# Nine panels on unnormalised x: the first norm's factor applied where the results are read

## The reference, cut to what matters

```
h = rms_norm(x, mix_norm_g)      # x * rsqrt(mean(x*x) + 1e-6) * g
proj = h @ w_in                  # 1024 x 7424
y_a = short_conv_mixer(proj[sc]); y_b = stick_breaking_attention(proj[sb])
y_c = rwkv7_mixer(proj[rw]);      y_d = spatial_gating(proj[sg])
gates = sigmoid(proj[gate] + gate_b)
```

## Time and profile before

| | us |
|---|---|
| median of three runs | 1012.99 |
| the profiled execution, whole | 1011.81 |
| its span, first to last instruction | 1010.0 |
| TensorE busy | 985.8 |
| VectorE busy | 695.9 |
| ScalarE busy | 537.2 |
| GpSimd busy | 35.5 |

### The profile page before, as it was taken

One profiled execution on the slowest core, in us unless ns is written; L12 is line 12 of the kernel. 1 busy time (PEld: TensorE's weight loads), 2 busy tenths in 40 slices (PEclk: granted clock), 3 DMA queues, 4 the chain that ended last, 5 costly groups with the idle time before them and its releaser, 6 DMA issues.

```text
span 1010.0 us, 20599 instructions
## 1 busy us (share of the span) xinstructions
PE 985.8 (98%) x8640; PEld 955.7 (95%) x8640; DVE 695.9 (69%) x855; ACT 537.2 (53%) x689; POOL 35.5 (4%) x28
## 2 busy tenths in 40 slices
PE   6998999999999999998999999999999999999998
PEld 5998898998999999998999999999999899999998
DVE  5678754655788988899886755556777867555553
ACT  5465645445565545466655444443676765435432
POOL 0035050000000000000000000000000000000000
PEclk9999999999999999999999999999999999999999
DMA  7643433332745555545333555555543135565551
GB/s 275 214 169 117 164 98 117 122 127 86 277 168 192 185 208 199 176 167 209 126 126 126 209 192 202 188 182 192 209 145 140 51 126 201 179 207 204 168 206 42
DMA packets 24833, 168.97 MB, mean 167 GB/s; under 512 B 2752, under 2 KB 3264, under 8 KB 4800
## 3 DMA queue, kind: packets, MB, share of 16 engines
q1 hardware_dynamic: 24192, 165.82, 46.9%
q10 hardware_dynamic: 576, 2.20, 0.6%
HBM read 166.96 MB, written 1.05 MB: 166 GB/s over the span
## 4 chain that ended last, share of the span: by engine, by line
PE 80%; DVE 13%; ACT 4%; issue 2%; DMA 0%; DVEq 0%; ACTq 0%
PE G L594 14%; PE G L595 13%; PE G L596 13%; PE D L594 8%; PE D L595 8%; PE D L596 8%; DVE wlo L1792 5%; PE M L595 2%; PE M L594 2%; PE M L596 2%; ACT whi L1275 2%; PE M L811 1%; PE D L1134 1%; PE D L1203 1%; PE M L641 1%
## 5 line engine op out<-in xcount | busy, mean ns | idle before, releaser
L1792 DVE TENSOR_TENSOR wlo<-raw,whi 128x2048 fp32r<-128x2048 f32 x155 | 354.2, 2290 | 125.7 <-ACT whi L1275 125.5
L594 PE MATMUL G<-xh,whi 128*128 128x256 f32 x1280 | 362.7, 283 | 4.4 <-DVE xl L1813 2.9
L595 PE MATMUL G<-xl,whi 128*128 128x256 f32 x1280 | 356.0, 278 | 0.0
L596 PE MATMUL G<-xh,wlo 128*128 128x256 f32 x1280 | 355.9, 278 | 0.0
L1275 ACT ACTIVATE whi<-raw 128x2048 fp32r<-128x2048 f32 x155 | 295.5, 1909 | 57.6 <-PE D L596 47.5
L594 PEld LDWEIGHTS G<-xh,whi 128*128 128x128 f32 x1280 | 241.8, 189 | 12.4 <-DVE wlo L1792 7.0
L595 PEld LDWEIGHTS G<-xl,whi 128*128 128x128 f32 x1280 | 241.6, 189 | 1.3 <-issue 1.2
L596 PEld LDWEIGHTS G<-xh,wlo 128*128 128x128 f32 x1280 | 241.5, 189 | 0.0
L594 PE MATMUL D<-hh,whi 128*128 128x256 f32 x672 | 185.8, 276 | 0.6 <-issue 0.6
L595 PE MATMUL D<-hl,whi 128*128 128x256 f32 x672 | 185.6, 276 | 0.0
L596 PE MATMUL D<-hh,wlo 128*128 128x256 f32 x672 | 185.6, 276 | 0.0
(11 more groups left out here) (398 smaller groups left out, 1383.5 us busy)
## 6 DMA issues: line engine op xcount, KB each, us to landing
raw<-wall_dram SPq DMA_DIRECT2D x155, 1024.0 KB, 4.9
x<-x_dram SPq DMA_DIRECT2D x4, 256.0 KB, 5.4
mem<-mem_dram ACTq DMA_DIRECT2D x1, 1024.0 KB, 4.8
out_dram<-x SPq DMA_DIRECT2D x4, 256.0 KB, 2.2
poolw<-pool_w_dram ACTq DMA_DIRECT2D x1, 768.0 KB, 6.3
cst<-cst_dram SPq DMA_DIRECT2D x1, 448.0 KB, 12.6
lora<-lora_dram SPq DMA_DIRECT2D x1, 256.0 KB, 11.9
sgw<-sg_w_dram SPq DMA_DIRECT2D x1, 256.0 KB, 12.7
```

Of the source, the lines that this page charges most:

```text
L594: mm(out, w_h, hi, start=start, stop=False, skip_group_check=skip)
L595: mm(out, w_h, lo, start=False, stop=False, skip_group_check=skip)
L596: return mm(out, w_l, hi, start=False, stop=stop, skip_group_check=skip)
L1792: signal(tt(wlo[:, pan.slot, 0:w], raw[:, pan.slot, 0:w], f32(whi[:, pan.slot, 0:w]), SUB), "w_lo")
```

## The change

The list starts with `gain` instead of `norm 0`. `gain` splits x * g (not x * g * rstd) into `gh` and `gl`, and panels 0 to 8 (rw, sc, sg) use these. The factor is applied when a result is read: for rw in a new VectorE step `rw_in`, in place after ScalarE's copy; for sc and sg by `read` on VectorE in place of ScalarE's copy. Squares are made after the splits, added on VectorE (`add_squares`, three instructions) and summed over channels by two fp32 products on TensorE. `root 0` comes after half of panel 1. The normalised x, which panels 9 and on still use, is made in five steps `norm_x` placed after panels 4 to 8. The load of panel 0 goes ahead of the four loads of x. `warm_start` runs first on TensorE. Three loads of constants share a semaphore, and some buffers move.

```diff
-    W = [("norm", 0)] + [("panel", PAN["rw"] + i) for i in range(4)]
-    W += [("rw_low",), ("panel", PAN["sc"]), ("rw_gates",), ("panel", PAN["sc"] + 1), ("rw_cum",), ("rw_square",),
-          ("panel", PAN["sc"] + 2), ("panel", PAN["sg"]), ("rw_key",), ("panel", PAN["sg"] + 1), ("rw_scale",), ("rw_mix",),
+    W = [("gain",), ("panel", PAN["rw"]), ("begin", PAN["rw"] + 1), ("root", 0), ("rw_in", 0)]
+    for i in range(1, 4):
+        W += [("panel", PAN["rw"] + i), ("rw_in", i)]
+    W += [("rw_low",), ("panel", PAN["sc"]), ("norm_x", 0), ("rw_gates",), ("panel", PAN["sc"] + 1), ("norm_x", 1), ("rw_cum",),
+          ("rw_square",), ("panel", PAN["sc"] + 2), ("norm_x", 2), ("panel", PAN["sg"]), ("norm_x", 3), ("rw_key",),
+          ("panel", PAN["sg"] + 1), ("norm_x", 4), ("rw_scale",), ("rw_mix",),
...
-    XLN = {"rw": 4, "wo": 8, ...
+    XLN = {"sb": 4, "wo": 8, ...
+    GAINED = ("rw", "sc", "sg")
+    SCALED = ("sc", "sg", "in0m", "kv")
...
+        load(Pan(0), A["wall"][0])
         for i in range(4):
             sp.dma_start(x[:, 2 * i:2 * i + 2, :], A["x"][:, 2 * i:2 * i + 2, :]).then_inc(S(f"x_moved{i}"), 16)
-        for p in range(SLOTS):
+        for p in range(1, SLOTS):
             load(Pan(p), A["wall"][p])
...
 # TensorE
+        def gained_panel(out, pan):
+            for i in range(4):
+                pe.wait_ge(S("gain_l"), i + 1)
+                for k in (2 * i, 2 * i + 1):
+                    for n in range(2):
+                        ins = tile3(out[:, n, :], pan, n * KT + k, P, gh[:, k, :], gl[:, k, :],
+                                    k == 0 and n == 0, k == KT - 1, skip=True)
+            return ins
...
-                for k in range(KT):
-                    pe.wait_ge(S("sq"), k // 2 + 1)
-                    ins = mm(M[1][:, 0, :], ones, wk[:, k, :], start=k == 0, stop=k == KT - 1)
+                ins = summed(M[1][:, 0, :], wk, "sq_sum", 0)
...
 # ScalarE
+        def gain():
+            split_to(1)
+            act.wait_ge(S("ld_par"), 16)
             for i in range(4):
+                act.wait_ge(S(f"x_moved{i}"), 16)
+                for k in (2 * i, 2 * i + 1):
+                    ins = fn(gh[:, k, :], x[:, k, :], ACT.Copy, scale=pcol("mix_g", k))
+                signal(ins, "gain_h")
+            split_to(2)
+            squares(0)
+
+        def norm_x(i):
+            if i < 4:
+                act.wait_ge(S("nrm"), i + 1)
                 signal(fn(xh[:, 2 * i:2 * i + 2, :], wk[:, 2 * i:2 * i + 2, :], ACT.Copy), "xh")
...
 # VectorE
+        def gain():
+            split_to(1)
+            for i in range(4):
+                dve.wait_ge(S("gain_h"), i + 1)
+                for k in (2 * i, 2 * i + 1):
+                    ins = stt(gl[:, k, :], x[:, k, :], pcol("mix_g", k), f32(gh[:, k, :]), MUL, SUB)
+                signal(ins, "gain_l")
+            split_to(2)
+            for i in (1, 2, 3):
+                add_squares(wk, "sq", 0, i, 3, "sq_sum")
+
+        def norm_x(i):
+            if i < 4:
+                scaled(wk, x, rstd, "mix_g", i, "nrm", 0)
+            if i:
+                low(i, i - 1, wk[:, 2 * i - 2:2 * i, :], xh, xl)
+
+        def rw_in(i):
+            projected(dve, "rw", i)
+            prs = slice(2 * i, 2 * i + 2)
+            own(tt(z_rw[:, prs, 1:T + 1], z_rw[:, prs, 1:T + 1], rstd[:].unsqueeze(1).broadcast_to([P, 2, T]), MUL))
+            own(tt(zs[:, prs, :], z_rw[:, prs, 0:T], z_rw[:, prs, 1:T + 1], SUB))
+            stt(zs[:, 2 * i, :], zs[:, 2 * i, :], pcol("mu", 2 * i), z_rw[:, 2 * i, 1:T + 1], MUL, ADD)
+            signal(stt(zs[:, 2 * i + 1, :], zs[:, 2 * i + 1, :], pcol("mu", 2 * i + 1),
+                       z_rw[:, 2 * i + 1, 1:T + 1], MUL, ADD), "rw_shift")
```

More of the change, by code:

```diff
@@ L193, in build @@
     merged = place("merged", [P, KT, T])
-    wk = place("wk", [P, KT, T], at=h_end["merged"] - 8 * K)
+    gl = place("gl", [P, KT, T], F32R, at=h_end["merged"] - 8 * K)
     cum = place("cum", [P, 4, P + 1])
@@ L220, in build @@
     hl1 = place("hl1", [P, 2, 2, T], F32R)
+    gh = place("gh", [P, KT, T], F32R, at=h_end["hl1"] - 10 * K + 384)
     top[0] = arena + 32
@@ L656, in norm_stat @@
             freed["M1"] = ("rs_read", n + 1)
-            if n == 0:
-                warm_start()
         def begin(p):
@@ L723, in panel @@
             w = P
-            if i == 0 and name in XLN:
+            if p == 0:
+                ins = gained_panel(out, pan)
+            elif i == 0 and name in XLN:
                 ins = first_panel(out, pan, XLN[name], a_h, a_l)
@@ L975, in sb_q @@
         def sb_q(h):
-            pe.wait_ge(S("ld_masks"), 16)
+            pe.wait_ge(S("ld_tables"), 48)
             pe.wait_ge(S("sb_sp"), h + 1)
@@ L1224, in pv_s @@
             freed[bank] = ("xl", 30 + g)
-        walk(pe, {"begin": begin, "quarter": quarter, "norm": norm_stat, "root": norm_stat, "panel": panel,
+        warm_start()
+        walk(pe, {"begin": begin, "quarter": quarter, "root": norm_stat, "panel": panel,
                   "rw_gates": rw_gates, "rw_key": rw_key, "rw_turn": rw_turn, "rw_prod": rw_prod,
@@ L1760, in out_s @@
             signal(fn(mh[:, 2 * g:2 * g + 2, :], BANK[SUMMED[g]][:, :, :], ACT.Copy), "xh")
-        walk(act, {"norm": norm, "squares": squares, "root": root, "parts": parts, "parts5b": parts5b, "panel": panel,
+        walk(act, {"gain": gain, "norm_x": norm_x, "squares": squares, "root": root, "parts": parts, "parts5b": parts5b, "panel": panel,
                    "rw_low": rw_low, "rw_gates": rw_gates, "rw_cum": rw_cum, "rw_key": rw_key,
@@ L1830, in root @@
             newton(rstd[:], M[1][:, 0, :], D, 1e-6, rtmp[:], ("rs_read", n + 1))
-        def norm(n):
-            root(n)
-            a, b, _, (gain, g0) = NORMS[n]
+        def gain():
+            split_to(1)
             for i in range(4):
[L1836 to L1840, removed]
+                dve.wait_ge(S("gain_h"), i + 1)
[18 more added lines that the diff above has]
+                       z_rw[:, 2 * i + 1, 1:T + 1], MUL, ADD), "rw_shift")
         def add_squares(buf, sem, before, i, last, done):
@@ L1858, in windows @@
         def windows(i):
-            dve.wait_ge(S("g_scaled"), i + 1)
+            projected(dve, "in0m", i)
             lo = 4 - 2 * i
@@ L1975, in panel @@
                                 merge_low(k - 1)
-            elif name == "kv":
+            elif name in ("kv", "sc", "sg"):
                 read(p)
[L1978 to L1984, removed]
         def read(p):
@@ L1992, in read @@
                 dst = zp[:, 4 - 2 * i:6 - 2 * i, 16:16 + T]
+            elif name == "kv":
+                dst = (ks, vs)[i][:, :, :]
             else:
-                dst = (ks, vs)[i][:, :, :]
+                dst = {"sc": z_sc, "sg": z_sg}[name][:, 2 * i:2 * i + 2, :]
             signal(tt(dst, G[gbank[p]][rows, :, :], rstd[rows, :].unsqueeze(1).broadcast_to([rows.stop, 2, T]), MUL),
@@ L2421, in _ @@
         dve.wait_ge(S("ld_cst"), 16)
-        walk(dve, {"norm": norm, "root": root, "final_norm": final_norm, "pool": windows, "add_sq": add_sq, "add_mem": add_mem, "parts": parts, "parts5b": parts5b,
+        walk(dve, {"gain": gain, "norm_x": norm_x, "rw_in": rw_in, "root": root, "final_norm": final_norm, "pool": windows, "add_sq": add_sq, "add_mem": add_mem, "parts": parts, "parts5b": parts5b,
                    "panel": panel, "rw_low": rw_low, "rw_gates": rw_gates, "rw_cum": rw_cum, "rw_key": rw_key, "rw_square": rw_square, "rw_scale": rw_scale,
```

40 lines of the change are left out of this document (11 added, 29 removed).

## The result

| | before | changed |
|---|---|---|
| median of four runs, us | 1011.15 (1009.00 to 1015.16) | 1024.45 (1017.68 to 1028.18) |
| ratio, 95% interval | | 1.011 [1.0072, 1.0148] |
| the profiled execution, whole | 1011.81 | 1017.68 |
| its span | 1010.0 | 1015.9 |
| panel 12 starts | 93.95 | 101.27 |

The change makes the kernel slower. The page's line of busy times answers to the earlier trace rows: TensorE is in flight 2.0 us less, VectorE is busy 11.0 us more, and the span is 5.9 us longer. So there is more standing still.

The account below looks back on a forecast made before the run. Bound: the start and VectorE's chain to panel 12, whose shift carries to the end. `rw_scale` 6.65 later, less 0.35 from GpSimd, is 6.3: 1011.8 + 6.3 = 1018.1, or 1019.3 by medians; said 1018.7, range 1009 to 1022.5.

Parts of the forecast that it names:

- Start: Up to panel 0: first product at 12.4, panel 0 ending at 18.05 instead of 23.6, a lead of 5.5 us.
- The factor and rw: `rstd` ready at 24.3, then VectorE without a wait through the rw panels to 40.0; `wlo` 6 done at 44.85.
- The lead is gone at panel 8: `whi` of panel 8 starts at 58.75, against 58.57 before, so nothing remains of the 5.5 us gained earlier.
- The ring: Panels 8 to 10: VectorE and ScalarE wait for each other in turn, so `rw_scale` begins 6.65 us later than 73.19.
- TensorE's waits: 2.2 us before panel 8, 6 us in panel 9, another before panel 11; all behind VectorE's chain, so not added.
- no GpSimd work lies beside a scaling: In this schedule VectorE's scalings of x never overlap GpSimd work, so the sum of 6.3 us later stays.
- 0.35 us come back: Behind the start of `rw_scale`, VectorE's line 1801 meets GpSimd differently: 0 to 1 us returns, 0.35 taken.
- the rule on GpSimd's shared interface: GpSimd shares VectorE's SBUF interface and contends with instructions having two SBUF inputs: bank reads safe, scalings not.
- Rival (a): TensorE keeps its 5.5 us from panel 0 because VectorE's chain is not the limit: 1006.3, or 1007.5 by medians; chance 0.13.
- (b): Up to panel 12, earlier landing of panel 0, GpSimd and shorter handovers leave 3 us of delay: about 1015; chance 0.25.
- Rival (c): Waits around panel 9 or a cold start put TensorE at 1.2 GHz: 1.65 to 2.8 us more, 1020 to 1022; chance 0.17.
- The comparison of totals: Whole kernel: 1018.1 against the profiled execution, 1019.3 beside the median 1.2 above it; 1018.7 said, between.

Follow-up runs that it names:

- the twelve later runs: The changed kernel once more, unaltered, beside the kernel before: median 1021.90 us, ratio 1.0071.
- the kernel before with the earlier high half: Kernel before, with ScalarE making the high half of panel 10 ahead of `rw_key`: 1010.39 us, ratio 0.9971; once more 1009.63 us, 0.9950.
- scalings and high half earlier: Changed kernel with the scalings a step earlier and the high half of panel 10 ahead of `rw_key`: 1008.72 us, ratio 0.9949; once more 1006.26 us, 0.9944.

## Why the prediction came out as it did

The mechanism was right, and nearly each step came at its time, the first of them by luck. The total lies above: the median of the four runs, 1024.45, is 5.8 us over my 1018.7 and 2 us over the upper end of the range; the twelve later runs (1021.9) are inside it. Over the 1012.99 that stood for the kernel before, 1018.7 is a ratio of 1.0056, under the first interval and inside the second.

- **Start.** First product at 12.42 (said 12.4), panel 0 5.7 us long at full clock. The time is right by luck: two errors cancel. Panel 0's `whi` began at 6.29, not at 7.4, so `gl` would have allowed 11.4; but the spare matmuls began at 6.51, released by the load of their constants, and not at 5.35, and held TensorE until 12.4, not 11.3. I had read a low level of TensorE from the spacing of the fp32 products; the granted clock of these stretches is 1.00 in both traces (5.35 to 8.00 before, 6.50 to 10.00 now), so that reading stays open.
- **The factor and rw.** `rstd` at 24.55 (24.3); VectorE went without a wait from there until 40.2 (40.0); `wlo` 6 ended at 45.1 (44.85). Right.
- **The lead is gone at panel 8.** Its high half began at 58.95 (58.75; 58.57 before). Right.
- **The ring.** `whi` 9 at 65.14 (64.9), `rw_key` 71.27 (71.15), `whi` 10 at 74.66 (74.5). Right, and the experiments show it as the cause: with the scaling earlier the whole loss goes, and a term of 0.6 us moves the ring by 0.6.
- **TensorE's waits.** 3.01 before panel 8 (2.2), 6.21 in panel 9 (6). Right. They aren't added, as said. The third, before panel 11, did not come: TensorE, at half rate from 80.61 to about 86, was itself not there before 92.08.
- **The step that failed: "no GpSimd work lies beside a scaling", and 0.35 us come back.** No scaling met GpSimd, but the last `xl` did (79.40, 1.16 us where it takes 0.68 alone), and line 1812 was as slow as before. `rw_scale` began 7.29 us later, not 6.65, and panel 12 7.32. Behind `rw_scale` GpSimd gave 0.8 back (0.85 for 1.66 at the second of the three instructions, line 1807 before) and took 0.9 (`wlo` 11, 3.38 for 2.48). In all it cost 0.5 us where I took 0.35 as a gain; the other 0.2 us of the 1.0 by which panel 12 missed 6.3 came ahead of `rw_scale` in pieces too small to place. I had checked the rule on GpSimd's shared interface for the scalings and not for the subtraction behind them.
- **Rival (a)**, the lead kept, is excluded by the traces, and **(b)** by panel 12.
- **Rival (c), the clock.** The wait in panel 9 brought 0.50 and it hid, as said. Where I feared 1.65 us more behind panel 12, 1.4 less came: the low stretch of the earlier trace rows was not there. I had carried it over unchanged in the sum, as if it belonged to the waits of 1.28 and 1.07. It doesn't belong to them alone: the kernel with the earlier scalings has the same two waits (1.27 and 1.07) and the granted clock behind them is 1.00, while with x loaded first the same two are followed by 0.61.
- **The comparison of totals.** I set the sum against two numbers 1.2 us apart and took their difference for the uncertainty of a run. The executions of one kernel lie further apart than the effect (below). Four runs of each gave 13.3 us between medians where the lowest runs differ by 8.7 here and 7.5 in the next group, and panel 12 by 7.3 and 6.3.

## What to carry to other kernels

Where two engines hand work to each other in a fixed order, idle time on either is not room: a turn of the ring is the sum of what stands between the handovers. Before adding a step that one engine makes and the other consumes, put the making ahead of the item that the other engine's next work waits for; here that one move of four scalings was worth about 7 us. And before an early start is paid for with work later, try the wait that limits the middle alone: one entry of a list gave all but about 1 us of what both together gave.

## What the runs showed of the hardware that was not expected

**Executions differ in the spacing of products at full clock.** These are the same 100 us in the first trace of the changed kernel and in the second (columns as in the earlier trace rows).

```profile
600.00:700.00 100.00, 100.00 (x884) 100.00 (x884) 55.37 (x37) 43.95 (x36) 0.00 (x0) 1.00 0.58 196
```

```profile
600.00:700.00 100.00, 100.00 (x851) 100.00 (x850) 52.92 (x36) 42.92 (x36) 0.00 (x0) 1.00 0.54 187
```

TensorE is never idle and the granted clock is 1.00 in both, yet one does 884 matmuls and the other 851: a product starts every 0.113 or every 0.118 us. From panel 12 to the end the first takes 914.6 us and the second 921.9. In this stretch all thirteen traces have either 884 or 885 matmuls (eight of them, before among them) or 851 or 852 (five). The same kernel can be on either side: so it is with the changed kernel here, and with the two executions of the kernel before with the earlier high half. Nor does an execution keep its spacing. In the second trace of the changed kernel it comes and goes:

```profile
400.00:440.00 40.00, 40.00 (x355) 40.00 (x354) 35.74 (x57) 21.43 (x28) 0.00 (x0) 1.00 0.54 184
600.00:640.00 40.00, 40.00 (x342) 40.00 (x341) 20.79 (x15) 17.06 (x15) 0.00 (x0) 1.00 0.58 204
900.00:940.00 40.00, 40.00 (x355) 40.00 (x354) 21.77 (x15) 19.42 (x16) 0.00 (x0) 1.00 0.54 184
```

The 35 runs of the kernel before in the first group lie at 1009.1 to 1013.1 (17 of them), 1015.0 to 1017.2 (15) and 1020.3 to 1021.5 (3). That the spacing makes these groups is likely but not shown, and what decides it, the runs don't show. With 12 runs against 35 the intervals of the ratio above are still 6 to 8 us wide; for a change of 5 us the lowest runs and the place of one instruction in the trace were the better readings.

**The clock after a wait.** Idle for 6.21, 6.22, 5.05 and 5.08 us, TensorE started again with products that took 0.55 to 0.58 us, at a granted clock of 0.50 to 0.53 behind it. The length of the wait alone doesn't decide it. After 2.82 us (scalings a step earlier) and after 3.01 us (changed kernel, 63.93) the clock stayed at 1.00:

```profile
73.26:78.00 4.74, 4.74 (x41) 4.74 (x42) 4.60 (x5) 2.83 (x3) 4.64 (x5) 1.00 0.47 197
```

But it fell behind a shorter one with x loaded first (0.50), and behind 2.57 us in the second trace of the changed kernel (0.67 from 62.90 to 67.00):

```profile
69.26 0.55 PE L601 MATMUL G<-gh,whi 128*128 128x256 f32 x1 [2.56 <-DVE z_sc L2018]
```

```profile
69.26:72.50 3.24, 3.24 (x15) 3.24 (x16) 1.35 (x4) 2.43 (x2) 0.00 (x0) 0.50 0.84 301
```

**GpSimd beside VectorE.** The instruction that began second was the one that took longer. In the changed kernel the split at 76.59 began first and took its usual 2.29 us, while GpSimd's multiplication, which takes 1.30 where nothing is in its way (72.11 in the first trace with scalings and high half earlier), took 3.34. The `xl` at 79.40 then began beside it and took 1.16 for 0.68; the read of a bank at 78.80, one of whose inputs is in PSUM, kept its 0.68.

```profile
76.67 3.34 POOL L576 TENSOR_TENSOR sgw<-sgw,cst 128x512 f32<-128x512 f32 x1
```

In that other trace GpSimd's addition at 85.05 began first and ended at 87.12, and the split at 85.89 took 3.38 us for 2.28. In each of these pairs the second took longer by about what was left of the first (the rest of 2.21 us for the multiplication, 0.61 for `xl`, 1.23 for the split). So a small shift of either engine decides which of them pays.
